# Rounding the merged tiles inside the third branch product of a hybrid diffusion step

## The reference, cut to what matters

```python
g = jax.nn.sigmoid(gates.reshape(b, t, N_BRANCH, D_MODEL))       # gates: last 3*1024 columns of h @ w_in
merged = (g[:, :, 0] * (oa @ p['w_branch_a']) + g[:, :, 1] * (ob @ p['w_branch_b'])
          + g[:, :, 2] * (oc @ p['w_branch_c']))
mix = merged @ p['w_o']
x = x + gate_m * mix                                             # then norm and the gated MLP
```

## Time and profile before

| | |
|---|---|
| median of 3 runs | 2822.33 us |
| the profiled execution itself | 2826.23 us |
| its span, first to last instruction | 2824.4 us |
| TensorE busy / weight loads | 91% / 82% of the span |
| VectorE / ScalarE / GpSimd busy | 49% / 35% / 14% |
| chain that ended last, by engine | PE 76%, issue 9%, DVE 7%, ACT 6%, POOL 2% |
| DMA | 202.75 MB, mean 72 GB/s |
| mean granted clock of TensorE | 0.948 of full speed |

### The profile page before, as it was taken

The page is one execution under the profiler, slowest core; times in us unless marked ns, Lnnn a source line. Parts: engine busy times, 40 slices in busy tenths (PEclk is TensorE's granted clock), DMA queues, the critical chain, the costliest instruction groups (busy, mean ns, idle before and its releaser), DMA issues.

```text
span 2824.4 us, 42887 instructions
## 1 busy us (share of the span) xinstructions
PE 2560.1 (91%) x17075; PEld 2309.6 (82%) x17075; DVE 1391.2 (49%) x2386; ACT 1000.0 (35%) x1721; POOL 404.8 (14%) x362
## 2 busy tenths in 40 slices
PE   6889989988988799999988999898989788999999
PEld 4768967687778799999976788666968688999998
DVE  3665256634644444334445743565357344442453
ACT  4343144413422444123243522453234225431332
POOL 0400031123010022012004000220220201210220
PEclk8999999999989899999989999998999899999999
DMA  6201213322121122232221012222210221222222
GB/s 217 86 19 46 81 60 129 120 73 68 61 61 61 51 75 67 69 87 70 65 82 53 31 60 66 70 75 75 64 60 31 75 75 45 74 70 79 74 58 84
DMA packets 252830, 202.75 MB, mean 72 GB/s; under 512 B 9876, under 2 KB 235910, under 8 KB 252678
## 3 DMA queue, kind: packets, MB, share of 16 engines
q1 hardware_dynamic: 245574, 197.67, 22.8%
q10 hardware_dynamic: 7104, 2.95, 0.4%
HBM read 196.50 MB, written 4.10 MB: 71 GB/s over the span
## 4 chain that ended last, share of the span: by engine, by line
PE 76%; issue 9%; DVE 7%; ACT 6%; POOL 2%; DMA 0%; POOLq 0%; ACTq 0%; DVEq 0%; SPq 0%
PE ps L1135 44%; PE ps L1287 5%; PE ps L1157 5%; PE ps L1299 3%; PE ps L1120 3%; PE ps L1121 3%; PE ps L1122 3%; PE ps L1326 3%; ACT prob L1564 2%; PE ps L1064 1%; PE ps L1230 1%; DVE wlo L1754 1%; PE ps L1247 1%; ACT hf L1420 1%; PE ps L1074 1%
## 5 line engine op out<-in xcount | busy, mean ns | idle before, releaser
L1754 DVE TENSOR_TENSOR wlo<-raw,whi 128x1024 fp32r<-128x1024 f32 (+4 forms) x288 | 362.5, 1260 | 554.8 <-ACT whi L1431 553.9
L1135 PE MATMUL ps<-hhi,whi 128*128 128x320 f32 x2048 | 479.8, 316 | 39.1 <-DVE hlo L1922 16.1
L1135 PE MATMUL ps<-hlo,whi 128*128 128x320 f32 x2048 | 474.3, 313 | 0.0
L1135 PE MATMUL ps<-hhi,wlo 128*128 128x320 f32 x2048 | 473.9, 313 | 0.0
L1431 ACT ACTIVATE whi<-raw 128x1024 fp32r<-128x1024 f32 (+4 forms) x288 | 281.2, 978 | 444.9 <-PE ps L1135 327.4
L1135 PEld LDWEIGHTS ps<-hhi,whi 128*128 128x128 f32 x2048 | 349.4, 192 | 48.9 <-issue 22.2
L1135 PEld LDWEIGHTS ps<-hlo,whi 128*128 128x128 f32 x2048 | 350.4, 192 | 0.0
L1135 PEld LDWEIGHTS ps<-hhi,wlo 128*128 128x128 f32 x2048 | 349.2, 191 | 0.0
L1828 DVE TENSOR_REDUCE negmax<-ps 128x1 f32<-128x640 f32 x192 | 151.9, 819 | 133.3 <-PE ps L1287 133.3
L2029 POOL TENSOR_TENSOR rstd<-smean,mhalf 128x4 f32<-128x4 f32 (+3 forms) x96 | 117.1, 1223 | 620.7 <-DVE smean L1804 620.5
L1120 PE MATMUL ps<-whi,hhi 128*128 128x512 f32 (+2 forms) x480 | 181.0, 377 | 12.2 <-issue 5.7
(11 more groups left out here) (205 smaller groups left out, 4245.7 us busy)
## 6 DMA issues: line engine op xcount, KB each, us to landing
raw<-in_w_up SPq DMA_DIRECT2D x88, 512.0 KB, 4.8
raw<-in_w_in SPq DMA_DIRECT2D x40, 1024.0 KB, 5.1
raw<-in_w_ada SPq DMA_DIRECT2D x40, 1024.0 KB, 5.2
raw<-in_w_down SPq DMA_DIRECT2D x16, 768.0 KB, 4.8
raw<-in_w_down SPq DMA_DIRECT2D x16, 640.0 KB, 4.4
adaw<-in_w_ada SPq DMA_DIRECT2D x8, 1024.0 KB, 10.6
raw<-in_w_o SPq DMA_DIRECT2D x8, 1024.0 KB, 5.1
raw<-in_w_branch_a SPq DMA_DIRECT2D x4, 1024.0 KB, 6.1
```

The costliest lines, as they stand in the source:

```text
L1135: mm = pe.matmul(out, w[:, sub, c], m[:, kt, o:o + HALF], start=first and i == 0 and a == 0, stop=last and i == len(ks) - 1 and a == 2)
L1754: dve.tensor_tensor(dst(wlo), src, dst(whi).bitcast(F32), ALU.subtract).then_inc(S["lo_ready"], 1)
```

## The change

The last two gate products of the third branch come ahead of its four product steps, and their weights are queued ahead of the branch weights. Gates 6 and 7 of this branch get a tensor of their own, `gatedC`, in memory that the third branch did not use. `msplit` now takes the tiles that it rounds: tiles 0 and 1 are rounded after the second product step, 2 and 3 after the third, and 4 to 7, with the merge of the fourth, behind the first weight split of the output projection. The wait on `mg_ready` is for the tiles at hand (`later` is how many of the additions counted so far it need not wait for). `zero` follows the second split. `load_gains` moves ahead of the third attention, and `gains` into its cycle 10 of 20 (counted from 0), ahead of the `score` step of that cycle. The other two branches keep their order.

```diff
     def branch(b):
         add("osplit", b=b)
+        if b == 2:
+            gate()
+            gate()
         for k in range(KD // 2):
-            if k == 2:
+            if k == 2 and b < 2:
                 gate()
                 gate()
             gemm("branch", b=b, k=k)
-            add("merge", b=b, k=k)
+            if b < 2 or k < KD // 2 - 1:
+                add("merge", b=b, k=k)
+            if b == 2 and 0 < k < KD // 2 - 1:
+                add("msplit", ks=(2 * k - 2, 2 * k - 1), later=2)
     def queue_branch(b):
+        if b == 2:
+            queue_gates(b, 6, 1)
         queue("branch", [SUB] * 2, b=b, u=0, cols=(4, 2 * P))
-        queue_gates(b, 6, 1)
+        if b < 2:
+            queue_gates(b, 6, 1)
         queue("branch", [SUB] * 2, b=b, u=1, cols=(4, 2 * P))
...
             add("params", of=at["l"] + 1)
+            add("load_gains", of=at["l"] + 1)
         attention("C", range(NH), [ada_steps, quarter_gates, quarter_gates, ada_steps, quarter_gates, quarter_gates,
-                                   ada_steps, ada_steps])
+                                   ada_steps, ada_steps],
+                  {-8: [dict(kind="gains", of=at["l"] + 1)]} if more else {})
...
             add("mod", part=0, of=at["l"] + 1)
-            add("load_gains", of=at["l"] + 1)
         branch(2)
-        if more:
-            add("gains", of=at["l"] + 1)
...
-        plan.extend(u[:2] + before[:1] + u[3:4] + before[1:] + list(between) + [u[2], u[4]])
+        plan.extend(u[:2] + list(early) + before[:1] + u[3:4] + before[1:] + list(between) + [u[2], u[4]])
...
     def ffn(l):
-        add("zero", what="wo")
-        left = fm_units("wo", KD // 2, SUB, [], [dict(step="msplit", l=l)], l=l)
+        last = [dict(step="merge", l=l, b=2, k=KD // 2 - 1)]
+        last += [dict(step="msplit", l=l, ks=(i, i + 1), later=KD - 2 - i) for i in (KD - 4, KD - 2)]
+        left = fm_units("wo", KD // 2, SUB, [], early=last, between=[dict(step="zero", l=l, what="wo")], l=l)
...
+        def gate_slot(b, g):
+            return gatedC[:, g - GATE_SLOTS, :] if b == 2 and g >= GATE_SLOTS else gated[:, g % GATE_SLOTS, :]
...
                 def msplit(s):                                    # ScalarE
-                    act.wait_ge(S["mg_ready"], n("mg_ready"))
-                    for k in range(KD):
+                    act.wait_ge(S["mg_ready"], n("mg_ready", -s["later"]))
+                    for k in s["ks"]:
                         act.activation(hhi[:, k, :], merged[:, k, :], ACT.Copy, scale=0.5).then_inc(S["mhi_ready"], 1)
...
                 def msplit(s):                                    # VectorE
-                    for k in range(KD):
-                        dve.wait_ge(S["mhi_ready"], n("mhi_ready", k + 1))
+                    for i, k in enumerate(s["ks"]):
+                        dve.wait_ge(S["mhi_ready"], n("mhi_ready", i + 1))
```

More of the change, by code:

```diff
@@ L225, in part @@
             else:
-                gemm("gate", g=count["gate"] % KD, ks=ks)
+                gemm("gate", g=count["gate"] % KD, b=count["gate"] // KD % 3, ks=ks)
                 count["gate"] += 1
@@ L239, in part @@
             prefetch(2)
-            step = dict(half=half, ks=ks, g=count["gate"] % KD, sub=count["gemm"] % 2, whole=i == 3)
+            step = dict(half=half, ks=ks, g=count["gate"] % KD, b=count["gate"] // KD % 3, sub=count["gemm"] % 2, whole=i == 3)
             if i == 3:
@@ L477, in mixers, with fm_units @@
             add("mod", part=0, of=at["l"] + 1)
-            add("load_gains", of=at["l"] + 1)
         branch(2)
-        if more:
-            add("gains", of=at["l"] + 1)
-    def fm_units(kind, n, width, before, between=(), lag=0, **k):
+    def fm_units(kind, n, width, before, between=(), lag=0, early=(), **k):
         assert not pending and count["gemm"] == count["split"]
@@ L670, in signals @@
     if k == "msplit":
-        return dict(mhi_ready=KD, mlo_ready=KD)
+        return dict(mhi_ready=len(s["ks"]), mlo_ready=len(s["ks"]))
     if k == "zero":
@@ L824, in program @@
                      ("qB", [P, 4, T], F32), ("kB", [P, 4, KEYS], F32), ("vB", [P, NK, 4, 64], F32)],
-                    [("qC", [P, 4, T], F32), ("kC", [P, KEYS], F32), ("vC", [P, NK, 128], F32)]]
+                    [("qC", [P, 4, T], F32), ("kC", [P, KEYS], F32), ("vC", [P, NK, 128], F32), ("gatedC", [P, 2, T], F32)]]
         ffn = [("ahi", [P, 12, T], F32R), ("alo", [P, 12, T], F32R), ("va", [P, 2, T], F32), ("vg", [P, 2, T], F32)]
@@ L832, in program @@
                     made += [st2.enter_context(nc.sbuf_tensor(*x)) for x in g]
-        (qA, kA, vA, bqT, ckvT, kpe, qB, kB, vB, qC, kC, vC) = made
+        (qA, kA, vA, bqT, ckvT, kpe, qB, kB, vB, qC, kC, vC, gatedC) = made
         size = max(sum(int(np.prod(x[1][1:])) for x in mixers + g) for g in branches)
         (ahi, alo, va, vg, adaw, room) = over(ffn, [("adaw", [P, ADA_FIRST // 2, 2 * SUB], F32)], [("mixroom", [P, size], F32)])
+        def gate_slot(b, g):
+            return gatedC[:, g - GATE_SLOTS, :] if b == 2 and g >= GATE_SLOTS else gated[:, g % GATE_SLOTS, :]
         cached = oT[:, :, :].rearrange("p a b -> p (a b)")
@@ L1536, in gate @@
                 def gate(s):
-                    slot = s["g"] % GATE_SLOTS
                     act.wait_ge(S["sub_done"], n("sub_done", 1))
@@ L1540, in gate @@
                     act.wait_ge(S["mg_ready"], n("mg_ready"))
-                    act.activation(gated[:, slot, :], run(3), ACT.Tanh, scale=0.5).then_inc(S["pair3_read"], 1)
+                    act.activation(gate_slot(s["b"], s["g"]), run(3), ACT.Tanh, scale=0.5).then_inc(S["pair3_read"], 1)
                 def gate_quarter(s):
@@ L1549, in gate_quarter @@
                         o = s["half"] * HALF
-                        act.activation(gated[:, s["g"] % GATE_SLOTS, o:o + HALF], bank(6)[:, OFF:], ACT.Tanh, scale=0.5)\
+                        act.activation(gate_slot(s["b"], s["g"])[:, o:o + HALF], bank(6)[:, OFF:], ACT.Tanh, scale=0.5)\
                            .then_inc(S["pair3_read"], 1)
@@ L1914, in merge @@
                         i = 2 * s["k"] + j
-                        g = gated[:, i % GATE_SLOTS, :]
+                        g = gate_slot(s["b"], i)
                         dve.scalar_tensor_tensor(out=g if s["b"] else merged[:, i, :], in0=g, scalar=1.0, in1=run(i % 3),
@@ L2046, in merge @@
                             pool.wait_ge(S["fm_read"], n("fm_read", j + 1))
-                            pool.tensor_tensor(merged[:, i, :], merged[:, i, :], gated[:, i % GATE_SLOTS, :], ALU.add)\
+                            pool.tensor_tensor(merged[:, i, :], merged[:, i, :], gate_slot(s["b"], i), ALU.add)\
                                 .then_inc(S["mg_ready"], 1)
```

## The result

The changed kernel takes 2800.76 us (median of 6 runs, 2795.99 to 2804.19) against 2822.68 (6 runs, 2821.62 to 2824.74) for the kernel before on the same chip: a ratio of 0.9915 (0.9904 to 0.9926), 21.9 us less. The forecast was 2799.2. The execution that was profiled is the shortest of the six, 2795.99 us with a span of 2794.2 and a mean granted clock of 0.956; that of before had 2826.23, 2824.4 and 0.948.

The account below looks back on a forecast made before the run. TensorE, 91% busy, was taken as the bound, so only its stalls near the changed steps counted; -5.7 - 1.8 + 0.4 - 12.75 + 0.3 - 4.8 + 1.2 = -23.1 gave 2799.2 us, bounds 2795 to 2803.

Parts of the forecast that it names:

- Parts 1 and 2: Start of third branch: gate weights land sooner, -5.7 us; gates need no `olo`, -1.8; lost half-clock luck, +0.4.
- the start stays: Rival: third branch begins no earlier, since issue time or a queue neighbour is late; 2806.7 us, chance 0.09.
- Part 3: Start of output projection: with rounding under the branch product, gaps shrink from 9.24 and 6.91 us to 1.7, -12.75.
- the +0.3 for a bad fit: VectorE's queue inside the third branch product: some tenths lost if its step doesn't quite fit, bounds 0 and 6 us.
- One of my signs of an error: Inside the third branch product: VectorE's `hlo` taking 2 us and more would show the prediction wrong.
- Part 4: Start of output projection: TensorE keeps full clock after standing only 1.7 us, -4.8 us, bounds 0 to -4.8.
- the clock falls all the same: Rival at the output projection: 1.7 us without matmuls suffice to drop the clock; 2804.0 us, chance 0.13.
- Part 5: First layer's third attention, near cycle 10: TensorE waits 1.2 us for the moved `gains`, bounds 0 and 2.
- that rival: Slower than before: `hlo` beside GpSimd stretch to 4.7 us, overfilling VectorE's steps in the third product; 2837.6 us, chance 0.03.

Follow-up runs that it names:

- the two halves: Changed kernel with the weights of gates 6 and 7 of the third branch loaded in two loads of 64 partitions instead of one: 2804.34 us, ratio 0.9937.
- the two filled gaps: From two runs of the changed kernel with ten unread matmuls on TensorE between last branch product and output projection: 2796.25 and 2796.75 us.
- two shortened to 0.96 us: Changed kernel with four PSUM pairs instead of three for the tiles of the third branch product: 2798.92 us, ratio 0.9907.
- two without a gap: Changed kernel with four PSUM pairs, the third branch's additions on VectorE, and tiles 4 and 5 rounded ahead of the last merge: 2794.80 us, ratio 0.9904.
- the one of 3.33 us: Changed kernel with `load_gains` and `gains` back in their old places, `gains` ahead of the last merge in VectorE's queue: 2804.84 us, ratio 0.9939.

## Why the prediction held, step by step

The forecast for the changed stretches was -23.1; three traces gave -21.8, -20.2 and -20.5. The whole kernel over 17 runs lies about 21 us under before. The mechanism was right and one term too large.

- *Parts 1 and 2, -7.1:* -7.4 measured alone, -6.7 in the changed kernel (-6.9 up to the first gate's start, and 0.1 more for the product). ScalarE's start 5.2 us behind the issue, the bracket of about 7 and the gate directly behind the last `mod` came as said, and the two halves took 4.4 us of it back. The rival "the start stays" is refuted by that: it was the kind of load.
- *Part 3, -12.75:* the gaps went from 16.15 to 3.7 us, -12.45; 1.85 each where I counted 1.7. The queue fitted with 0.65 us to spare in a step, where the prediction had 0.2; the +0.3 for a bad fit was not needed. TensorE idles nowhere inside the branch product itself. The Trainium skill, SBUF — State Buffer, "Who interferes with whom", foresaw the taking of turns, and the traces agree: two `hlo` beside GpSimd take 3.79 us, and 1.55 with GpSimd's additions taken away. One of my signs of an error came up all the same: the second `hlo` of each pair takes 2.18 us, over the 2 us that I had named (1.9 is only the mean of the two). It was the wrong sign, for the step still had room.
- *Part 4, -4.8, is the step that was mis-sized.* I took 1.85 us as safe because 0.84 had been, with nothing between. The trace of the kernel before had gaps between: behind one of 1.74 us the granted clock was 1.00 from 332 to 336 us, and behind one of 1.67, with two of 1.1 to 1.2 us shortly ahead of it, it was 0.50 from 417 to 423 us. In the changed kernel the clock fell behind four of six gaps, and the two first output tiles take 16.3 us together on average, 18.9 before: the term is -2.6. The rival "the clock falls all the same" is half true; it had priced the whole loss at 4.8, but a fall behind 1.85 us costs 1.5, and those behind 9.24 and 6.91 us had cost 2.0 and 2.6 by the same measure. That the gap is the cause rests on the two filled gaps behind a short first gate product (8.55 and 8.93 us), where the clock stayed. The other six places with no fall (two filled, two shortened to 0.96 us, two without a gap) stood behind 9.18 to 10.05 us. In five of them (9.51 and more) the clock would probably have stayed behind 1.85 us too, as in the five cases above, so they prove nothing, and 0.96 us isn't shown to be safe.
- *Part 5, +1.2:* 1.0 measured, of which 0.79 is one idle time of TensorE, in the kernel before with this part alone and in the changed one.

The measured terms are -6.7 - 12.45 - 2.6 + 1.0 = -20.8, the mean of the three traces. No `hlo` came near 3.4 us, where that rival would have decided. That the profiled execution of after came out at 2795.99, 6.7 us under the median of its 17 runs, was mostly luck in the untouched rest.

## What to carry to other kernels

Look at what stands last in the queues when a product ends: work that needs only earlier tiles of the result can be put under the product, and the gap shrinks to what truly needs the last tile; then count, for each engine, whether a step has room for it, with the stretched durations that two engines beside each other show. Where a load is awaited, put one there that lands quickly, and keep the slow kind for a place with cover. A gap on TensorE costs more than its length if the clock falls behind it, and it may fall in one execution and not in the next, so one trace of such a stretch is not enough. Look also at how long the clock was half ahead of the stretch: here a part of the loss only moved from one place to the other.

## What the runs showed of the hardware

- TensorE's granted clock is not sure behind a short stop: after a gap of 1.85 us in full work it fell from 1.0 to 0.5 in 6 of 11 cases, each for a loss of 1.5 us; after the one of 3.33 us it fell, and after 0.18 us (4 cases) and 0.96 us (2 cases) it didn't.
- The 6 cases are those in which the first 48 matmuls of the product, begun at half clock, took 8.55 to 9.05 us; in the other 5 they took 9.53 to 10.07.
- Two loads of 64 partitions and 512 KB each took 7.4 us from issue to the first use, one load of 128 partitions and 1024 KB 5.2 us, at the same place and time.
- VectorE did two of GpSimd's additions and two `hlo` in 3.1 us, less than the 3.79 us that the two `hlo` alone took beside GpSimd's additions.
- The same 7,700 matmuls between the two layers took 1260 to 1268 us from one execution to the next, with equal work on the other engines; the difference is time at 1.2 GHz. Single executions of the changed kernel lie up to 11.7 us apart (2795.56 to 2807.24), more than any of the smaller edits here is worth.
